# Sliding attention in a three-block network: one row of scores per query, the sink as a column, deeper buffers, the norm's scale moved into the rotation's tables

## The chip, the cores and the metric

The kernel is one program on one core of a Trainium2 chip. It has five engines that run their own instruction streams and meet only at semaphores: TensorE (PE; its weight loads are PEld), VectorE (DVE), ScalarE (ACT), GpSimd (POOL) and SyncE (SP, which here only starts the loads of weights). The metric is the device time of one execution in microseconds (us).

## The reference, cut to what matters

Three blocks in a row work on 256 tokens of width 1024. The change touches the third block, in which 16 meta tokens stand in front of the 256 (272 in all), and there the mixer of its second layer: attention in a sliding window, 16 query heads of 64, four heads of keys and values, and a sink (one learned number per head) in the softmax.

```python
def sink_softmax(s, mask, sink):
    s = jnp.where(mask, s.astype(jnp.float32), NEG_INF)
    m = jnp.maximum(jnp.max(s, axis=-1, keepdims=True), sink)
    p = jnp.exp(s - m)
    return p / (jnp.sum(p, axis=-1, keepdims=True) + jnp.exp(sink - m))

def swa_mixer(hn, w_q, sinks, w_out, k, v, cos, sin):     # hn = rmsnorm(h) * gain
    q = (hn @ w_q).reshape(B, L, N_KV_HEADS, GROUP, HEAD_DIM)
    q = (apply_partial_rope(q, cos, sin) * (HEAD_DIM ** -0.5)).transpose(0, 2, 3, 1, 4)
    ...
    mask = jnp.concatenate([
        jnp.ones((nB, WINDOW_3, N_META), dtype=bool),
        (j > i)[None] & (blk > 0),
        jnp.broadcast_to((j <= i)[None], (nB, WINDOW_3, WINDOW_3)),
    ], axis=-1)
    p = sink_softmax(s, mask, sink_b[None, :, :, None, None, None])
    o_real = jnp.einsum('bkgnqs,bknsd->bkgnqd', p.astype(v.dtype), v_band)
```

The window is 128. A query in the second half of the 256 tokens sees, of the first half's 128 keys, those with j > i, and of its own half's those with j <= i: for each query the two masks never take the same column, so the two halves together have exactly 128 visible keys, beside the 16 meta keys.

## The kernel before, in words

The whole network is a list of stages in `build`; each stage has one method per engine (`pe`, `act`, `dve`, `pool`), and the engines run the stages in order. Activations lie transposed, feature by token. Products with large weights are exact to fp32 by three fp32r products (`mm3`: high by high, low by high, high by low); every 128x1024 unit of weights is loaded by SP into one of 8 raw slots, its high part is copied by ACT (`W.hi`, tile `hi`, 5 slots in a ring, or a `spare` slot), and its low part is computed by DVE (`W.lo`) or, for every third unit, by POOL (`W.lo_pool`). Small products of attention are plain fp32.

A stage begins with an entry, which applies the last stage's update to `xT` and norms it. There are two kinds in play here. `Full`: eight tiles are updated (DVE, two operations each) and squared (ACT); PE sums the squares, DVE and POOL compute the inverse root, PE spreads it over the partitions; only then DVE makes x * gain * scale (tile `sq`), ACT its high part `hh` and DVE its low part `hl`, and the first product of the stage follows. `Lazy` (the entry of most feed-forward stages): `hh` and `hl` are made of x * gain as soon as a tile is updated, the products run on them, and the norm's sums and scale come after the first product, in the shadow; the scale is applied to the products.

`Swa` (from line 3678) is the stage that is changed; its entry is `Full`. Eight units of query weights give eight pairs of heads (u = 0 to 7). `first` computes two of them, `lin` one each in iterations 1, 3, 5, 7, 9 and 11 of the loop. A pair's query goes PE product, ACT (`query`, scale 1/8, tile `qs`), then the rotation (`Rope`): PE multiplies by a permutation, POOL multiplies `qs` by the cosines, DVE the permuted one by the sines, DVE adds (`rotated`, signal `rq`). Attention runs over 16 windows w: pair u = w // 2, half m = w % 2, both heads r of the pair at a time. The loop over i (`for i in range(21)`) is a software pipeline written out by hand; every engine takes its part of the windows in a fixed order:

- PE in iteration i: `scores(i)`, `lin` when it is due, `turn(i-3)` (transposes of the probabilities), the permutation, `values(i-5)`;
- ACT: copies of the products of window i-6 out (tile `sqr`), copies of the transposes of window i-4 out, `exps(i-1)`, `query`;
- DVE: `probs(i-2)`, `rowmax(i)`, `W.lo`, `rotated`, the low part of the output of window i-6 (tile `swal`, signal `ol`).

For m = 1 a row of scores has 272 columns (two halves and 16 meta keys), for m = 0 144. `rowmax` adds the mask for each head, takes the maximum, the maximum with the sink, its negative, and sink minus maximum: six instructions, in which each small one waits for the one before. `exps` takes the exponential of the sink and of two rows with their sums. `probs` adds the sink's term, takes the reciprocal and scales the two rows. The scores have two banks for each of two windows; the output of `values` has one bank, so that `values(w)` waits for `ol(w-1)`:

```python
        pe.wait_ge(*self.pta(w))
        if w:
            pe.wait_ge(*self.ol(w - 1))
```

The 16 meta queries go through a small path of their own (`meta_scores`, `meta_max`, `meta_probs`, `meta_turn`, `meta_values`). After the loop comes the output product (`Down`), whose first instruction waits for `ol(15)`.

Of the kernel before, what the change touches and what calls it, by code (L numbers as in the profile page):

```python
# [31 lines left out]
def table(sizes):  # L32
# [22 lines left out]
    ("chunk", 2), ("level", 320), ("mask64", 128), ("id64", 64), ("nlow", 64), ("nup", 64), ("tri128", 128), ("suf128", 128), ("swa", 272), ("cos", 272), ("sin", 272), ("turn", 128),  # L55
# [3 lines left out]
def constants():  # L59
# [216 lines left out]
class K:  # L276


    def __init__(self, nc, ctx, d, out):
# [19 lines left out]
        self.small, _ = self.place("small", 512)  # L299
        self.NA = (nc.sbuf_usable_end - self.at) // 4 // 16 * 16  # L300
        self.A, self.Aat = self.place("arena", self.NA)
        self.ps = [ctx.enter_context(nc.psum_tensor(f"ps{i}", [P, 512], F32)) for i in range(8)]
# [356 lines left out]
class Lazy:  # L659


    def __init__(self, K, T, prev, gain, j):
        self.K, self.T, self.prev = K, T, prev
        self.gain = lambda k: K.col(gain, j * 8 + k)
        self.hh, self.hl, self.sq, self.pr, self.rs = [
            K.sig(*a) for a in (("hh", 8), ("hl", 8), ("sq", 8), ("pair", 4), ("rstd", 1))]
# [2907 lines left out]
class Rope:  # L3574
# [10 lines left out]
    def pool(self, pool, j, src, t1):  # L3585
        pool.wait_ge(*self.qs(j))
        pool.tt(t1, src, self.K.c("cos"), ALU.mult).then_inc(self.t1.h, 1)

    def dve(self, dve, j, t2, bank):
        dve.wait_ge(*self.rm(j))  # L3590
        dve.tt(t2, bank[:, 0:T3], self.K.c("sin"), ALU.mult).then_inc(self.t2.h, 1)
        dve.wait_ge(*self.t2(j))
        dve.wait_ge(*self.t1(j))


class Shared(Mixer):
# [30 lines left out]
    def act(self, act):  # L3627
# [7 lines left out]
        act.act(self.V[:, 0, :], ps[0][:, 0:256], ACT.Copy)  # L3635
        act.act(self.V[0:16, 2, :], ps[7][0:16, 0:256], ACT.Copy).then_inc(self.va.h, 1)

    def dve(self, dve):
# [5 lines left out]
        for j in range(2):  # L3644
            t1, t2 = self.t1[:, j, :], self.t2[:, j, :]
            self.rope.dve(dve, j, t2, ps[4 + 2 * j])
# [8 lines left out]
    def pool(self, pool):  # L3655
# [6 lines left out]
        for j in range(2):  # L3662
            self.rope.pool(pool, j, self.fm[:, j, :], self.t1[:, j, :])
# [14 lines left out]
class Swa(Mixer):  # L3678

    def __init__(self, K, entry, exit_):
# [6 lines left out]
        self.S = buf(8 * T, 4, 2, T)  # L3689
        self.PT = buf(2 * 4 * P, 2, 4, P)  # L3690
        self.PM = buf(2 * 2 * P, 2, 2, P)
        self.qs, self.t1, self.t2 = [buf(2 * T, 2, T) for _ in range(3)]
# [5 lines left out]
        self.rq = sg("sw_q", 8)  # L3698
        self.sc, self.mx, self.es, self.ex, self.pr, self.tr, self.pta, self.pv, self.oh, self.ol = [
            K.sig(x, 16) for x in ("scores", "rowmax", "sink", "exps", "probs", "turned", "pta", "pv", "oh", "ol")]  # L3700
        (self.m0, self.m1, self.m2, self.m3, self.m4, self.m5, self.m6, self.m7, self.m8, self.mh) = [
            sg("sw_m" + str(i), 1) for i in range(10)]
        self.st = [[K.small[:, 64 * i + 16 * x:64 * i + 16 * x + 2] for x in range(3)] for i in range(4)]
        self.st2 = [K.small[0:16, 320 + 16 * x:336 + 16 * x] for x in range(3)]
        self.down = Down(K, T, "swa_out", self.mix, 8, lambda k: self.ol(2 * k + 1), spare=K.spare)
# [3 lines left out]
    KEYS = (((0, P), (T1, 16)), ((0, T3),))  # L3709
    WIDE = (144, 272)  # L3710
# [3 lines left out]
    def pe(self, pe):  # L3714
        K, ps, T = self.K, self.K.ps, T3
        self.entry.pe(pe)
        self.first(pe, self.u, (ps[7], ps[6]), K.HL, T, self.entry.hl)
# [3 lines left out]
        for i in range(21):  # L3721
            if i < 16:
                self.scores(pe, i)
            if i % 2 and i < 12:
# [5 lines left out]
            if i % 2 == 0 and 0 < i < 14:  # L3730
                j = (i + 2) // 2
                self.rope.pe(pe, j, self.qs[:, j % 2, :], self.product(j))
            if i > 4:
                self.values(pe, i - 5)
            if i == 13:
                self.meta_scores(pe)
            if i == 16:
                self.meta_turn(pe)
            if i == 18:
# [6 lines left out]
    def product(self, j):  # L3746
        return self.K.ps[4 + j if j < 2 else 7]

    def meta_scores(self, pe):
        K = self.K  # L3750
        pe.wait_ge(*self.rq(7))
        pe.wait_ge(*self.mx(12))
        for h in range(16):
            o = 64 * (h % 2)
            t = pe.mm(K.ps[h % 2][0:16, h // 2 * 16:h // 2 * 16 + 16], self.qT[o:o + 64, h // 2, T1:T3],
                      self.kD[o:o + 64, h // 4, T1:T3])
# [18 lines left out]
    def scores(self, pe, w):  # L3775
        K, u, m = self.K, w // 2, w % 2
        pe.wait_ge(*self.rq(u))
        if w > 1:
            pe.wait_ge(*self.mx(w - 2))
        if w == 14:  # L3780
            pe.wait_ge(*self.m1(0))
        for r in range(2):
            o, at = 64 * r, 0
            for c, n in self.KEYS[m]:
                t = pe.mm(K.ps[w % 2 * 2 + r][:, at:at + n], self.qT[o:o + 64, u, m * P:(m + 1) * P],
                          self.kD[o:o + 64, u // 2, c:c + n])
                at += n
        t.then_inc(self.sc.h, 1)

    def turn(self, pe, w):  # L3790
        K, u, m = self.K, w // 2, w % 2
# [3 lines left out]
        else:  # L3795
            pe.wait_ge(*self.rope.t2(1))
        for r in range(2):
            for c in range(m + 1):
                at = (r * (m + 1) + c) * P
                pe.tr(K.ps[4][:, at:at + P], self.S[:, w % 4, r, c * P:(c + 1) * P], K.ident)  # L3800
            c = P * (m + 1)
            t = pe.tr(K.ps[5][0:16, r * P:(r + 1) * P], self.S[:, w % 4, r, c:c + 16], K.ident)
        t.then_inc(self.tr.h, 1)

    def out(self, w):
        return self.K.ps[6][:, 0:P]

    def values(self, pe, w):
        K, u, m = self.K, w // 2, w % 2
        kv = u // 2 * 64  # L3810
        pe.wait_ge(*self.pta(w))
        if w:
            pe.wait_ge(*self.ol(w - 1))
# [383 lines left out]
```

## Time and profile before

| what | value |
|---|---|
| time, median of 3 runs | 3581.78 us (3574.05 to 3582.15) |
| time of the profiled execution | 3582.93 us |
| its span | 3581.1 us |
| mean granted TensorE clock | 0.925 of full |
| PE busy | 3283.6 us (92%) |
| DVE, ACT, POOL busy | 1808.7, 1526.3, 912.4 us |

The span is what the profiler saw from first to last instruction; 1.8 us of the time lie around it. Granted clock: TensorE runs at one of two levels, 1.2 GHz (0.50) and 2.4 GHz (1.00); a stretch between them was partly at either. All helper calls carry the line of the helper (L158 is `tt`, L162 `ts`, L166 `stt`, L172 `red`, L175 `act`, L178 `mm`, L186 `tr`), so operations are told apart by their tiles. A plain fp32 matmul shows as two records, a transpose and an fp32r matmul as one; some records are missing from the trace.

### The profile page before, as it was taken

Reading aid. Unit: us, or ns where it says so; the run is one execution under the profiler, and the core shown is the slowest. Engines: PE = TensorE matmul, PEld = TensorE weight load, DVE = VectorE, ACT = ScalarE, POOL = GpSimd, SP = SyncE. Lnnn points to the kernel's source line nnn. Section 1 sums busy time; section 2 is a strip of 40 time slices with the busy share of each in tenths; the row PEclk is TensorE's granted clock in tenths of the full one; section 3 lists DMA queues with packets and bytes.
Section 4 is the critical chain, followed back from the end, with each engine's and each line's share of the span. In section 5 each row is a group of like instructions: output and inputs, shape, how many; then the busy total and the mean of one; then the engine's idle time right before and its main releaser. Section 6 shows DMA issues by size and latency. Waiting matters only on the chain.

```text
span 3581.1 us, 63633 instructions
## 1 busy us (share of the span) xinstructions
PE 3283.6 (92%) x27126; PEld 3135.0 (88%) x27126; DVE 1808.7 (51%) x3157; ACT 1526.3 (43%) x2540; POOL 912.4 (25%) x474
## 2 busy tenths in 40 slices
PE   9998999989788999989969999999899979977998
PEld 9996999987678999988858899899799979975898
DVE  5446555558565454474655344544435454454443
ACT  5444444434124444356454344443334443432442
POOL 3221222322342323212202122222122222220222
PEclk9988999989898999989979999999899989986899
DMA  6541454544003555533414345354224524520353
GB/s 229 187 150 59 147 184 164 184 164 147 31 3 129 178 171 188 172 111 116 148 42 152 116 163 188 132 176 138 89 83 154 176 100 160 177 83 18 109 175 118
DMA packets 133385, 484.43 MB, mean 135 GB/s; under 512 B 14959, under 2 KB 17151, under 8 KB 132399
## 3 DMA queue, kind: packets, MB, share of 16 engines
q1 hardware_dynamic: 131120, 470.25, 38.9%
q0 software_dynamic: 1984, 10.12, 0.9%
q8 instruction: 214, 3.51, 0.4%
q14 instruction: 67, 0.55, 0.0%
HBM read 479.27 MB, written 1.05 MB: 134 GB/s over the span
## 4 chain that ended last, share of the span: by engine, by line
PE 81%; DVE 9%; ACT 5%; issue 3%; POOL 1%; DMA 0%; DVEq 0%; POOLq 0%; ACTq 0%
PE ps L178 80%; ACT hi L175 1%; DVE lo L158 1%; ACT arena L175 1%; PE ps L186 1%; DVE arena L158 1%; POOL small L158 1%; DVE tmp L166 1%; DVE yT L166 1%; DVE arena L166 1%; ACT L175 1%; DVE small L172 1%; ACT xT L175 0%; ACT hh L175 0%; DVE hl L158 0%
## 5 line engine op out<-in xcount | busy, mean ns | idle before, releaser
L178 PE MATMUL ps<-hh,lo 128*128 128x256 f32 (+1 forms) x4624 | 1342.8, 290 | 0.0
L178 PE MATMUL ps<-hh,hi 128*128 128x256 f32 (+1 forms) x4336 | 1273.9, 294 | 74.5 <-DVE hl L166 33.2
L178 PE MATMUL ps<-hl,hi 128*128 128x256 f32 (+1 forms) x4336 | 1261.1, 291 | 0.0
L158 POOL TENSOR_TENSOR lo<-raw,hi 128x1024 fp32r<-128x1024 f32 x271 | 687.3, 2536 | 1893.2 <-ACT hi L175 1893.1
L175 ACT ACTIVATE hi<-raw 128x1024 fp32r<-128x1024 f32 x814 | 852.5, 1051 | 462.8 <-PE ps L178 341.9
L158 DVE TENSOR_TENSOR lo<-raw,hi 128x1024 fp32r<-128x1024 f32 x543 | 699.0, 1290 | 603.3 <-ACT hi L175 582.5
L178 PEld LDWEIGHTS ps<-hh,hi 128*128 128x128 f32 x4336 | 851.1, 196 | 91.1 <-DVE hl L166 24.2
L178 PEld LDWEIGHTS ps<-hh,lo 128*128 128x128 f32 x4624 | 904.5, 196 | 0.0
L178 PEld LDWEIGHTS ps<-hl,hi 128*128 128x128 f32 x4336 | 849.2, 196 | 0.2
L178 PE MATMUL ps<-hfh,lo 128*128 128x256 f32 (+1 forms) x1760 | 499.7, 284 | 0.0
L178 PE MATMUL ps<-hfh,hi 128*128 128x256 f32 (+1 forms) x1520 | 431.2, 284 | 0.0
L178 PE MATMUL ps<-hfl,hi 128*128 128x256 f32 (+1 forms) x1520 | 430.9, 283 | 0.0
L178 PEld LDWEIGHTS ps<-hfh,lo 128*128 128x128 f32 x1760 | 331.6, 188 | 0.0
L178 PE MATMUL ps<-arena 64*64 64x64 f32 (+10 forms) x2992 | 257.6, 276 | 66.6 <-DVE sqr L158 18.0
L178 PEld LDWEIGHTS ps<-arena 64*64 64x64 f32 (+5 forms) x2992 | 193.1, 162 | 124.0 <-issue 40.2
L178 PEld LDWEIGHTS ps<-hfl,hi 128*128 128x128 f32 x1520 | 286.7, 189 | 0.0
L178 PEld LDWEIGHTS ps<-hfh,hi 128*128 128x128 f32 x1520 | 286.4, 188 | 0.0
L158 DVE TENSOR_TENSOR tmp<-tmp,ps 128x256 f32<-128x256 f32 (+1 forms) x220 | 94.0, 427 | 334.6 <-PE ps L178 313.8
L175 ACT ACTIVATE arena<-ps 128x256 f32<-128x256 f32 (+6 forms) x300 | 117.6, 412 | 292.3 <-PE ps L178 224.7
L175 ACT ACTIVATE hfh<-tmp 128x256 fp32r<-128x256 f32 (+1 forms) x220 | 93.0, 423 | 297.4 <-DVE tmp L158 295.9
L158 DVE TENSOR_TENSOR hfl<-tmp,hfh 128x256 fp32r<-128x256 f32 (+1 forms) x220 | 128.0, 582 | 125.8 <-ACT hfh L175 125.8
L175 ACT ACTIVATE tmp<-tmp 128x256 f32<-128x256 f32 (+1 forms) x176 | 74.8, 425 | 244.7 <-DVE tmp L158 244.7
(351 smaller groups left out, 3859.6 us busy)
## 6 DMA issues: line engine op xcount, KB each, us to landing
raw<-in_l_ffn_w_gate SPq DMA_DIRECT2D x88, 512.0 KB, 3.5
raw<-in_l_ffn_w_up SPq DMA_DIRECT2D x88, 512.0 KB, 4.0
raw<-in_l_ffn_w_down SPq DMA_DIRECT2D x88, 512.0 KB, 4.2
raw<-in_g SPq DMA_DIRECT2D x88, 512.0 KB, 3.3
raw<-in_u SPq DMA_DIRECT2D x88, 512.0 KB, 3.3
raw<-in_d SPq DMA_DIRECT2D x88, 512.0 KB, 3.3
raw<-in_ffn_w_gate SPq DMA_DIRECT2D x44, 512.0 KB, 4.3
raw<-in_ffn_w_up SPq DMA_DIRECT2D x44, 512.0 KB, 4.3
```

The source lines that it names most:

```text
L158: return self.e.tensor_tensor(o, a, b, op)
L166: return self.e.scalar_tensor_tensor(o, a, s, b, op0, op1)
L172: return self.e.tensor_reduce(o, a, AX_X, op)
L175: return self.e.activation(o, a, f, **kw)
L178: return self.e.matmul(o, a, b, start=first, stop=final, skip_group_check=loose)
L186: return self.e.transpose(o, a, ident)
```

## The change

- The entry of `Swa` becomes `Lazy`. `first` computes four query pairs at once, from banks 0 to 3; then come the norm's sums, two permutations, and `spread`. DVE multiplies the tables of cosines and sines by the norm's scale (tiles `cos`, `sin` of the stage), and the rotations use these. `lin` is left in iterations 5, 7, 9 and 11.
- Scores: the meta keys have columns of their own; for m = 1 the keys of the other half go to columns 256 to 383 of the bank. DVE adds the mask to both heads in one instruction and, for m = 1, writes the other half's scores over the masked columns (`copy_predicated`). Both halves' keys so share one row of 128. The sink stands as a column of the row (written once by POOL), so that one `tensor_reduce` with `negate` gives the negative maximum of both heads and the exponential's sum holds the sink's term.
- `probs`: a reciprocal and one multiplication over both heads. `turn`: three transposes for every window. For m = 1 the transposed probabilities are multiplied by one mask on DVE (`PN`) and by the other on POOL (`PB`), and `values` reads these.
- Buffers: 16 rows instead of 4 for scores, four for the transposes, four for `qs`, two output banks; `values(w)` waits for `ol(w-2)` and runs as `values(i-6)`; the loop has 23 iterations on PE and 24 on ACT and DVE.
- The stage `Shared` copies the meta values a second time (partitions 32 to 47). The constants grow from 272 to 288 + 128 columns for the masks. PSUM is one tensor of eight banks. The output product's last three units use spare slots of the stage's own.

```diff
-    keep = np.concatenate([j > i, j <= i, np.ones((P, 16), bool)], 1)
+    keep = np.concatenate([j <= i, np.ones((P, 32), bool), j <= i], 1)
     put("swa", np.where(keep, 0.0, BIG))
+    put("swab", j > i)
...
+        act.act(self.V[32:48, 2, :], ps[7][0:16, 0:256], ACT.Copy)
...
     def pe(self, pe):
-        self.entry.pe(pe)
-        self.first(pe, self.u, (ps[7], ps[6]), K.HL, T, self.entry.hl)
+        self.first(pe, self.u, ps[0:4], K.HL, T, self.entry.hl)
+        self.entry.norm.sums(pe, [(2 * i, self.entry.pr(i)) for i in range(4)])
         K.enter.have(pe)
         for j in range(2):
             self.rope.pe(pe, j, self.qs[:, j, :], self.product(j))
-        for i in range(21):
+        self.entry.norm.spread(pe)
+        for j in (2, 3):
+            pe.wait_ge(*self.rope.t2(j - 2))
+            self.rope.pe(pe, j, self.qs[:, j, :], self.product(j))
+        for i in range(23):
             if i < 16:
                 self.scores(pe, i)
-            if i % 2 and i < 12:
+            if i % 2 and 4 < i < 12:
...
-            if i > 4:
-                self.values(pe, i - 5)
+            if i > 5 and i - 6 < 16:
+                self.values(pe, i - 6)
...
-        for r in range(2):
-            o, at = 64 * r, 0
-            for c, n in self.KEYS[m]:
-                t = pe.mm(K.ps[w % 2 * 2 + r][:, at:at + n], self.qT[o:o + 64, u, m * P:(m + 1) * P],
+        parts = ((0, 16), m * P, P), ((P, 0), T1, 16), ((256, 256), 0, P)
+        for at, c, n in parts[:2 + m]:
+            for r in range(2):
+                o = 64 * r
+                t = pe.mm(self.K.ps[w % 2 * 2 + r][:, at[r]:at[r] + n], self.qT[o:o + 64, u, m * P:(m + 1) * P],
                           self.kD[o:o + 64, u // 2, c:c + n])
...
         for r in range(2):
-            for c in range(m + 1):
-                at = (r * (m + 1) + c) * P
-                pe.tr(K.ps[4][:, at:at + P], self.S[:, w % 4, r, c * P:(c + 1) * P], K.ident)
-            c = P * (m + 1)
-            t = pe.tr(K.ps[5][0:16, r * P:(r + 1) * P], self.S[:, w % 4, r, c:c + 16], K.ident)
+            pe.tr(b[:, r * P:(r + 1) * P], self.row(w)[:, 176 * r:176 * r + P], self.K.ident)
+        t = pe.tr(b[0:48, 256:384], self.row(w)[:, P:176], self.K.ident)
...
-        if w:
-            pe.wait_ge(*self.ol(w - 1))
+        if m:
+            pe.wait_ge(*self.mn(u))
+            pe.wait_ge(*self.mb(u))
+        if w > 1:
+            pe.wait_ge(*self.ol(w - 2))
...
+        dve.wait_ge(*self.entry.norm.spr(0))
+        dve.mark(dve.tt(self.cos, K.c("cos"), self.entry.norm.out, ALU.mult))
+        dve.tt(self.sin, K.c("sin"), self.entry.norm.out, ALU.mult).then_inc(self.tb.h, 1)
+        dve.wait_ge(*self.tb(0))
...
+    def masked(self, e, u, to, mask, done):
+        e.wait_ge(*self.pta(2 * u + 1))
+        if u > 1:
+            e.wait_ge(*self.pv(2 * u - 3))
+        e.tt(to[:, u % 2, :].rearrange("p (r t) -> p r t", r=2),
+             self.PT[:, (2 * u + 1) % 4, :].rearrange("p (r t) -> p r t", r=2),
+             bc_mid(self.K.c(mask), 2), ALU.mult).then_inc(done.h, 1)
...
-        for r in range(2):
-            dve.mark(dve.tt(self.S[:, w % 4, r, 0:n], K.ps[w % 2 * 2 + r][:, 0:n], K.c("swa")[:, 272 - n:272], ALU.add))
-        dve.turn()
-        dve.mark(dve.red(mx, self.S[:, w % 4, :, 0:n], ALU.max))
-        dve.turn()
-        dve.mark(dve.tt(mx, mx, sink, ALU.max))
-        dve.turn()
-        dve.mark(dve.ts(mx, mx, -1.0, None, ALU.mult))
-        dve.turn()
-        dve.tt(e, sink, mx, ALU.add).then_inc(self.mx.h, 1)
+        b = K.banks[:, w % 2 * 2:w % 2 * 2 + 2, :]
+        dve.mark(dve.tt(self.two(S, 160, 144), b[:, :, 0:144],
+                        K.c("swa").rearrange("p (r c) -> p r c", r=2), ALU.add))
+        dve.turn()
+        if m:
+            dve.mark(dve.e.copy_predicated(self.two(S, 176, P), bc_mid(K.c("swab").bitcast(mybir.dt.uint32), 2),
+                                           b[:, :, 256:384]))
+            dve.turn()
+        dve.e.tensor_reduce(mx, self.two(S, 159, 145), AX_X, ALU.max, negate=True).then_inc(self.mx.h, 1)
...
-        lambda p: Swa(K, Full(K, T3, p, "norm_gains_3", 8), rms("norm_gains_3", 9, False, False, K.Hf)),
+        lambda p: Swa(K, Lazy(K, T3, p, "norm_gains_3", 8, False), rms("norm_gains_3", 9, False, False, K.Hf)),
```

## Rows read from the trace of the kernel before

**Rows 1.** The page, part 4: the chain that ended last, by engine.
```profile
PE 81%; DVE 9%; ACT 5%; issue 3%; POOL 1%; DMA 0%; DVEq 0%; POOLq 0%; ACTq 0%
```
**Rows 2.** Windows: stretch, its length, busy us (instructions) by engine, PEclk, DMA share, GB/s.
```profile
3165.28:3188.85 23.57, 18.96 (x101) 18.33 (x102) 13.46 (x34) 6.86 (x17) 1.20 (x2) 0.56 0.00 1
3188.85:3219.93 31.08, 20.65 (x129) 16.78 (x128) 22.21 (x61) 13.03 (x38) 8.60 (x6) 0.84 0.19 68
3219.93:3264.19 44.26, 35.80 (x206) 26.18 (x205) 21.94 (x75) 15.40 (x54) 4.59 (x4) 0.81 0.11 37
3264.19:3324.60 60.41, 46.68 (x249) 27.73 (x247) 19.47 (x73) 15.87 (x58) 0.76 (x1) 0.53 0.03 9
...
3312.03:3319.52 7.49, 7.49 (x53) 5.07 (x52) 0.29 (x1) 1.28 (x4) 0.00 (x0) 0.50 0.01 2
```
**Rows 3.** The chain in order of time, stage's entry and two `lin`: start, us, what.
```profile
3175.81 1.21 POOL small L158 x2
...
3177.07 1.77 PE ps L178 x6
...
3207.09 4.55 PE ps L178 x24
...
3216.81 3.31 PE ps L178 x24
```
**Rows 4.** Waits of PE, 3219 to 3325 us: total us, times, longest.
```profile
PE ps L178 <- DVE swal L158: 17.8, 11, 2.6
PE ps L186 <- ACT arena L175: 3.9, 6, 1.0
```
**Rows 5.** Timeline of DVE and PE in the next stage's `Lazy` entry (four units).
```profile
3356.90 0.50 DVE L166 SCALAR_TENSOR_TENSOR yT<-yT,cols,ps 128x272 f32<-128x272 f32 x1 [2.41 <-PE ps L178]
...
3373.58 2.50 PE L178 MATMUL ps<-cst,sq 128*128 128x1 f32 x22
```
**Rows 6.** Groups by shape, DVE, ACT, POOL: count, busy us, mean ns, idle before.
```profile
L158 DVE TENSOR_TENSOR lo<-raw,hi 128x1024 fp32r<-128x1024 f32 x543 | 699.0, 1290 | 603.3 <-ACT hi L175 582.5
...
L158 DVE TENSOR_TENSOR arena<-ps,cst 128x272 f32<-128x272 f32 x24 | 9.8, 435 | 17.8 <-PE ps L178 17.8
L158 DVE TENSOR_TENSOR arena<-arena 128x272 f32<-128x272 f32 x8 | 4.0, 500 | 0.6 <-POOL arena L158 0.4
L172 DVE TENSOR_REDUCE small<-arena 128x2 f32<-128x288 f32 x8 | 3.6, 453 | 0.3
...
L3520 DVE COPY_PREDICATED arena<-cst,ps 128x128 f32<-128x128 uint32 x8 | 2.0, 298 | 7.6 <-PE ps L178 7.6
...
L175 ACT ACTIVATE arena<-ps 128x256 f32<-128x256 f32 x8 | 3.0, 378 | 0.0
...
L158 POOL TENSOR_TENSOR lo<-raw,hi 128x1024 fp32r<-128x1024 f32 x3 | 7.1, 2354 | 41.3 <-ACT hi L175 41.3
L158 POOL TENSOR_TENSOR arena<-arena,cst 128x272 f32<-128x272 f32 x8 | 7.0, 880 | 33.4 <-ACT arena L175 33.4
```
**Rows 7.** Timeline of PE late in the loop: start, us, what [idle before <-releaser].
```profile
3280.91 3.08 PE L178 MATMUL ps<-arena 128*64 128x128 f32 x40 [1.38 <-DVE swal L158]
3284.57 1.04 PE L178 MATMUL ps<-arena 64*128 64x128 f32 x8 [0.58 <-DVE arena L158]
...
3288.26 4.60 PE L178 MATMUL ps<-arena 128*64 128x128 f32 x16 [1.17 <-DVE swal L158]
3292.84 1.09 PE L186 MATMUL ps<-cst,arena 128*128 128x128 f32 x4
3296.53 2.54 PE L178 MATMUL ps<-arena 128*64 128x128 f32 x8 [2.61 <-DVE swal L158]
3300.04 1.51 PE L186 MATMUL ps<-cst,arena 128*128 128x128 f32 x6 [0.97 <-ACT arena L175]
...
3320.30 3.36 PE L178 MATMUL ps<-arena 128*64 128x128 f32 x12 [0.78 <-DVE swal L158]
```
**Rows 8.** Timeline of DVE beside a running low-part subtraction on POOL.
```profile
3213.75 1.73 DVE L158 TENSOR_TENSOR small<-small,rows 128x2 f32<-128x2 f32 x1
```

More of the change, by code:

```diff
@@ L298, in __init__ @@
         self.tmp = p3(self.place("tmp", 4 * T3)[0][:, :], 4)
-        self.small, _ = self.place("small", 512)
+        self.small, _ = self.place("small", 464)
         self.NA = (nc.sbuf_usable_end - self.at) // 4 // 16 * 16
         self.A, self.Aat = self.place("arena", self.NA)
-        self.ps = [ctx.enter_context(nc.psum_tensor(f"ps{i}", [P, 512], F32)) for i in range(8)]
+        self.banks = ctx.enter_context(nc.psum_tensor("ps", [P, 8, 512], F32))
+        self.ps = [self.banks[:, i, :] for i in range(8)]
         self.ident, self.ones = self.c("ident"), self.c("ones")
@@ L3751, in meta_scores @@
         pe.wait_ge(*self.rq(7))
[L3752 to L3756, printed above, removed]
+        for r in range(2):
+            for u in range(8):
+                o, h = 64 * r, 2 * u + r
+                t = pe.mm(K.ps[7][0:16, h * 16:h * 16 + 16], self.qT[o:o + 64, u, T1:T3],
+                          self.kD[o:o + 64, u // 2, T1:T3])
+            if r == 0:
+                pe.mark(t)
+                pe.turn()
         t.then_inc(self.m0.h, 1)
@@ L3827, in act @@
         self.entry.act(act)
-        for j in range(2):
-            self.query(act, j, ps[7 - j])
-        for i in range(22):
-            if i > 5:
-                w = i - 6
+        for j in range(4):
+            self.query(act, j, ps[j])
+        for i in range(24):
+            if i > 6 and i - 7 < 16:
+                w = i - 7
                 act.wait_ge(*self.pv(w))
@@ L3949, in probs @@
-        t.then_inc(self.pr.h, 1)
+        s = self.two(self.row(w), 160, 144)
+        dve.tt(s, s, bc(den, 144), ALU.mult).then_inc(self.pr.h, 1)
     def meta_max(self, dve):
@@ L3983, in pool @@
         K, W = self.K, self.K.W
-        pool.wait_ge(*K.enter.loaded())
+        K.enter.all(pool)
         K.enter.tables(pool)
         K.enter.have(pool)
+        if self.u:
+            pool.wait_ge(*W.used(self.u - 1))
+        rows = self.S[:, 0:16 * 304].rearrange("p (u m c) -> p m u c", m=2, c=304)
+        pool.e.memset(self.S[:, 0:16 * 304].rearrange("p (w c) -> p w c", c=304)[:, :, 144:160], 0.0).then_inc(self.pad.h, 1)
+        pool.wait_ge(*self.pad(0))
+        sinks = K.row("swa_sinks_3").rearrange("p (u r) -> p r u", r=2)
+        for r in range(2):
+            for m in range(2):
+                t = pool.cp(rows[:, m, :, self.SINK[r]], sinks[:, r])
+        t.then_inc(self.snk.h, 1)
         self.entry.pool(pool)
+        self.entry.norm.power(pool)
+        W.lo_pool(pool, self.u + 6)
+        pool.wait_ge(*self.tb(0))
         for j in range(8):
+            self.rope.pool(pool, j, self.qs[:, j % 4, :], self.t1[:, j % 4, :], self.cos)
             W.lo_pool(pool, self.u + j + 6)
-            self.rope.pool(pool, j, self.qs[:, j % 2, :], self.t1[:, j % 2, :])
+            if j > 3:
+                self.masked(pool, j - 4, self.PB, "suf128", self.mb)
+        for u in range(4, 8):
+            self.masked(pool, u, self.PB, "suf128", self.mb)
         self.down.pool(pool)
```

177 lines of the change are left out of this document (91 added, 86 removed).

## The prediction, made before the changed kernel was run

> **What bounds the kernel now.** I read the page first: the chain that ended last lies for 81% on PE [rows 1], so time comes off only where PE waits, runs at the low clock, or has work that goes away. The stage that changes runs from the first update of `xT` (3165.28 us) to the first product of `Down` (3324.60): 159.3 us, which I cut with the windows view into an entry, the loop up to the end of `lin` in iteration 5 (3219.93), up to the end of the last `lin` in iteration 11 (3264.19), and a tail without dense products [rows 2]. The reader should see that the four parts have different limits. The entry, 23.6 us, is a round trip: PE sums the squares as the updates go on, then come inverse root and spread (1.21 and 1.77 us) [rows 3], then DVE makes the normed tiles before a product can start. In the loop, PE is busy 36 of 44 us and 47 of 60 us. The waits view says what the rest is: 17.8 us in eleven waits for `swal`, that is for `ol(w-1)`, and 3.9 us for ACT's copies of the transposes [rows 4]. The wait for `ol` is a ring: `values(w)` fills the one output bank, PE does `scores`, DVE does the whole of `rowmax` for these scores first (its order is written by hand) and only then `ol(w)`, which frees the bank. The tail is PE at half clock: 0.53 on average, and 0.50 even in 7.5 us in which PE never stopped [rows 2]. So there every product counts double.
>
> **The change, part by part.** I lay out a new time line from 3165.28, where the stage starts as before.
>
> *Entry.* The next stage has the new kind of entry, with four units too: from its first update (3356.90) to the start of the norm's sums (3373.58) are 16.7 us [rows 5]. That puts the end of the four products at 3182.0, with two more pairs of heads done than before had at 3188.85. Then the sums 2.5 us [rows 5], variance 0.3, inverse root 1.2 and spread: 1.8 at half clock [rows 3], 0.9 at full; I take 1.3: 3187.3. DVE's two tables at 0.44 (PSUM by constant, 272 columns [rows 6]) end at 3188.2. Then four rotations: POOL is behind them with 0.8 to 0.88 each [rows 6], and the last addition follows: 3192.2. All this is on the path, because `rowmax(0)` stands behind the four rotations in DVE's order.
>
> *First iterations.* New `rowmax`: addition over 288 columns 0.46 (the 272 wide one is 0.435), reduction 0.45, so 0.95 with the gaps; for m = 1 also the predicated copy of 256 columns, 0.43 (0.298 for 128, and another 128 columns at the slope of about 1 ns of the additions) [rows 6]: 1.4. `probs`: a reciprocal on two columns and one multiplication over 288 (0.50 for the 272 wide addition, some of it waiting [rows 6]): 0.5 together. In DVE's order: `rowmax(0)` to 3193.2, `rowmax(1)` to 3194.6, two low-part subtractions of 1.25 (1.29 on average over the kernel [rows 6]; iteration 1 now has both) to 3197.1, `probs(0)` and `rowmax(2)` to 3198.5, `probs(1)` and `rowmax(3)` to 3200.5. `scores(5)` needs that last one; then `lin` of iteration 5, which after a wait costs 4.55 and not 3.31 [rows 3]: it ends at about 3205.6. Before that point was 3219.93. Saved: **14.3 us** (12 to 17: the clock in the four products, and DVE's gaps).
>
> *Iterations 6 to 11.* Three pairs of windows took 44.26 us, 14.8 a pair, clock 0.81 [rows 2]. New work of PE for a pair, from rows at half clock [rows 7]: `values` 2.54 (m = 0, eight records) and 3.36 (m = 1, twelve), unchanged. `turn`: four transposes take 1.09, six 1.51, so 0.21 for one more, and three take 0.88, twice 1.76 in place of 2.60. `scores` m = 0: eight records 1.04, at most as before. `scores` m = 1: 4.60 less 3.36 is 1.24 for two products of 272 columns; the new one has four of 128 and two of 16, which I put between 1.0 and 2.0, at 1.5. Together 10.2 at half, 5.1 at full clock; with `lin` (3.31 at full) and a permutation (one product of 272 columns, an estimate from the 1.24 for two: 0.9 at half, 0.45 at full) 8.9 at full. At the old mix of clocks (0.81) that is 10.9. The ring is gone: `values(w)` waits for `ol(w-2)`, which has a whole iteration to come. What is late next is `pta`: ACT does the output's copy and two copies (0.38 for the longest [rows 6]) before `turn` may go on, about 0.95 us from the end of `values`, and PE has only `scores` to fill it: 0.3 a window, 0.6 a pair. 11.5 a pair, 34.5 for three. Saved: **9.8 us** (16 if the clock holds full: 8.9 + 0.6 + 0 = 9.5 a pair; 4 if it falls to 0.70: 8.9 / 0.70 + 0.6 = 13.3).
>
> *Tail.* At half clock, from the end of the last `lin`: eight `turn` 7.0; six `values` of m = 1 and five of m = 0 (windows 5 to 15, one window more than before, since `values` now runs an iteration later) 20.2 + 12.7; four `scores` 2 × 1.04 + 2 × 1.5 = 5.1; one permutation 1.0; the meta path 0.6 for its scores (3.08 less 2.54 [rows 7]), an estimated 2.2 for its other products (as many, some wider); the first `turn` and `values(5)` still at full clock, less 2.1; then waits for `pta`: 0.3 in four iterations, 0.97 in three without `scores` (as now [rows 7]), 4.1; and 0.95 from the last `values` to `Down`. Sum 51.8. Now it is 60.4. Saved: **8.6 us**, I take 8 (4 to 13: `scores` dearer, a mask late, or a part at full clock).
>
> *What costs nothing.* DVE has about 3.0 + 3.1 us of work a pair (two `rowmax` 2.35, two `probs` 1.0, `rotated` 0.9, `PN` 0.45, `ol` 0.6, a subtraction 0.8) against PE's 11: PE covers it. ACT has under 6. POOL's masks (0.88 at most) for window 2u+1 wait for ACT's copy in iteration 2u+5 and are needed in iteration 2u+7, so two windows of PE hide them. The sinks are written by POOL in the entry, where it waits for DVE. More constants load in the first blocks' shadow. The second copy of the meta values in `Shared` is on the path: ACT makes it before the copy that PE waits for, **+0.3 us**.
>
> *A rule beside the rows.* A DVE operation on two columns took 1.73 us [rows 8], longer than a reduction of 288 columns (0.453), while a subtraction of 2.35 us ran on POOL [rows 6]. The Trainium skill (SBUF — State Buffer, "Who interferes with whom") says that a DVE instruction with two SBUF inputs and a GpSimd one that reads SBUF exclude each other for the whole instruction; the trace agrees with 1.73 us. By that rule eight new POOL masks could stop DVE for up to 8 × 0.88 = 7.0 us; without it for nothing. Neither changes the sum while PE covers DVE. By itself: the Trainium skill (TensorEngine Tiling, "Key Properties") says that row tiles work independently, by which the interleaved heads' scores would come out near the 1.0 end; no row here shows it.
>
> **Sum.** 14.3 + 9.8 + 8.0 - 0.3 = 31.8 us. The profiled execution took 3582.93 us (1.8 around its span), 1.2 above the median shown; so the new one should be about 3551 and the median **3550 us**, 0.9% less.
>
> **Rivals.**
> - *The clock stays at half in the whole loop.* Dense products lift it; two of six `lin` leave the loop, and the entry's pauses are shorter but still there. The tail at 0.50 with PE at work [rows 2] speaks for it; that a `lin` ran in 3.31 us and the mean there is 0.81 [rows 2, 3] speaks against. Then: four products 8 us longer, `lin` of iteration 5 1.2 longer, a pair 6.6 + 0.9 + 10.2 + 0.6 = 18.3, three of them 55 against 44.3. 14.3 - 9.2 - 10.7 + 8 - 0.3 = 2 saved: 3580 us, no change. Chance 7%.
> - *The clock holds at full through most of the loop*, because the waits of 1 to 2.6 us go. 14.3 + 16 + 8 + up to 10 in the tail: 3533 to 3543 us. The 7.5 us at 0.50 speak only against rising, not against staying. Chance 15%.
> - *DVE becomes the bound (the slower side).* The row views are strided, the predicated copy reads PSUM, and POOL's masks block it. It decides when DVE needs more than PE's 11.5 a pair; to eat all 32 us over eight pairs it must need 15.5, that is 9.4 more than I count, 1.2 us on each of eight operations. One blocked by a subtraction for 1.7 us in a pair is what rows 8 show, not five. At 17 a pair: 3594 us. Chance 4%.
> - *A part of the gain is missing* (rotations or `pta` longer, scores at 2.0): 15 to 22 saved, 3560 to 3567 us. Chance 14%.
>
> **Chances and range.** My forecast, 3543 to 3558, has 60%. The range of 8 in 10 takes in most of the third and second rival: 3534 to 3568. 0.3% is 10.7 us, about what a measurement of this kernel can tell from no change. Faster by more: forecast, full clock and smaller gain, 88% (I give one point to no change); within: 8%; slower: 4%.
>
> **What would show it.** The first product of the stage under the updates of `xT`, and the last of the four units' near 3182; `lin` of iteration 5 ending near 3205; no wait of PE for `swal` in the loop; `turn` with three transposes, 0.9 us at half clock; the tail near 52 us at 0.50 to 0.55; DVE groups of 0.45 us in place of the small ones. It would be wrong if the span from 3182 to the first `scores` is much over 10 us, if PE waits for DVE's maxima or for a mask in every iteration, or if the granted clock in the middle is under 0.7.

## The result and the profile after

Four runs of the changed kernel have a median of 3532.24 us (3527.84 to 3535.96), four of the kernel before 3579.14 us. The ratio is 0.9864 with a 95% interval of 0.9850 to 0.9877: 1.4% faster, 47 us on medians, where 31.8 had been forecast. The direction is right, the size is 1.5 times the forecast, and the time lies 1.8 us under the range of 3534 to 3568.

The windows view of the changed kernel, cut at the same events as before: first update of `xT`, end of the four units, end of `lin` in iteration 5, end of the last `lin`, first product of `Down`. Columns as in [rows 2]; the second part is given in two pieces, split at 3190.30, and the last two rows split the tail behind the fall of the clock.

```profile
3163.60:3179.44 15.84, 13.48 (x97) 13.49 (x98) 11.69 (x28) 7.67 (x18) 0.00 (x0) 0.83 0.01 2
3179.44:3190.30 10.86, 8.99 (x46) 6.19 (x45) 4.60 (x13) 5.39 (x8) 7.49 (x8) 0.65 0.52 193
3190.30:3207.40 17.10, 14.11 (x90) 12.31 (x89) 12.87 (x26) 5.39 (x24) 1.84 (x1) 0.53 0.00 1
3207.40:3235.06 27.66, 25.94 (x207) 20.25 (x205) 17.18 (x42) 12.72 (x47) 6.70 (x7) 1.00 0.17 58
3235.06:3278.30 43.24, 39.48 (x258) 24.35 (x257) 17.66 (x52) 13.41 (x54) 4.96 (x6) 0.64 0.04 13
3235.06:3249.40 14.34, 13.62 (x127) 9.24 (x126) 9.93 (x28) 7.32 (x30) 3.03 (x4) 0.93 0.12 39
3249.40:3278.30 28.90, 25.86 (x132) 15.11 (x133) 7.73 (x26) 6.09 (x24) 1.93 (x2) 0.50 0.00 1
```

The middle ran at 1.00 where it had 0.81 [rows 2], and the tail kept the high clock for its first 12 us. By parts, against the forecast's own time line:

| part | before | forecast | after | saved |
|---|---|---|---|---|
| first update to end of `lin` in iteration 5 | 54.6 | 40.3 | 43.8 | 10.8 (14.3 forecast) |
| to the end of the last `lin` | 44.3 | 34.5 | 27.7 | 16.6 (9.8) |
| tail, to `Down` | 60.4 | 52.4 | 43.2 | 17.2 (8.0) |
| stage | 159.3 | 127.2 | 114.7 | 44.6 |

The two spans differ by 47.0 us (3581.1 and 3534.1). The other 2.4 lie outside the stage, 1.7 of them ahead of it; profiled executions differ there by more than that (last section). The waits of PE in the loop of the changed kernel, columns as in [rows 4]:

```profile
PE ps L187 <- ACT arena L176: 4.8, 9, 1.1
PE ps L179 <- DVE small L3981: 1.4, 2, 1.2
PE ps L187 <- DVE arena L159: 1.2, 1, 1.2
```

`swal` is gone from the list. What is left is `pta` (nine waits, the longest 1.1 us) and, in the loop's first iterations, three waits for DVE's first maxima and probabilities. The timeline of PE late in the loop and in the tail, to be read against [rows 7]:

```profile
3235.32 2.50 PE L179 MATMUL ps<-arena 128*64 128x128 f32 x20
3238.14 0.52 PE L187 MATMUL ps<-cst,arena 128*128 128x128 f32 x3 [0.33 <-ACT arena L176]
...
3245.16 4.22 PE L179 MATMUL ps<-arena 128*64 128x128 f32 x52
3249.31 0.90 PE L187 MATMUL ps<-cst,arena 128*128 128x128 f32 x3
3250.14 3.39 PE L179 MATMUL ps<-arena 128*64 128x128 f32 x12
3254.41 0.88 PE L187 MATMUL ps<-cst,arena 128*128 128x128 f32 x3 [0.88 <-ACT arena L176]
3255.22 2.54 PE L179 MATMUL ps<-arena 128*64 128x128 f32 x8
...
3264.51 12.86 PE L179 MATMUL ps<-arena 128*64 128x128 f32 x72
```

Three transposes take 0.88 us at half clock and 0.52 or less at full; twelve records of `values` take 3.39 (3.36 before) and eight 2.54, as before. The last row of the timeline is 12.9 us of such products without a pause, all of it in a stretch at 0.50. The level had fallen 12.3 us after the last `lin` (full for 0.86 of the 14.34 us at 0.93), with no wait of PE longer than 0.33 us since. The groups by shape of DVE and POOL, for the prices that the forecast had to estimate:

```profile
L159 DVE TENSOR_TENSOR arena<-arena,small 128x288 f32<-128x288 f32 x16 | 7.3, 458 | 0.6
L3981 DVE TENSOR_REDUCE small<-arena 128x2 f32<-128x290 f32 x16 | 7.3, 455 | 0.6
...
L159 DVE TENSOR_TENSOR arena<-ps,cst 128x288 f32<-128x288 f32 x16 | 7.2, 451 | 4.8 <-PE ps L179 4.7
L159 DVE TENSOR_TENSOR arena<-arena 128x272 f32<-128x272 f32 x8 | 5.9, 733 | 0.7 <-POOL arena L159 0.5
...
L3978 DVE COPY_PREDICATED arena<-cst,ps 128x256 f32<-128x256 uint32 x8 | 3.6, 446 | 0.3
```
```profile
L159 POOL TENSOR_TENSOR arena<-arena,cst 128x256 f32<-128x256 f32 x8 | 6.4, 802 | 28.3 <-ACT arena L176 28.3
```

They came out as priced (0.451, 0.446, 0.455 and 0.458 us; POOL's masks 0.80). The one that didn't is the rotation's addition: 0.733 us on average, mainly because one of the eight was held (2.12 us; the first took 0.91, the last four 0.44). The timelines of POOL and DVE at that place:

```profile
3186.33 3.31 POOL L159 TENSOR_TENSOR arena<-arena 128x272 f32<-128x272 f32 x4 [0.41 <-DVE arena L159]
3189.59 2.55 POOL L159 TENSOR_TENSOR lo<-raw,hi 128x1024 fp32r<-128x1024 f32 x1
```
```profile
3190.32 2.12 DVE L159 TENSOR_TENSOR arena<-arena 128x272 f32<-128x272 f32 x1
3192.36 0.44 DVE L159 TENSOR_TENSOR arena<-ps,cst 128x288 f32<-128x288 f32 x1
3192.84 0.45 DVE L3981 TENSOR_REDUCE small<-arena 128x2 f32<-128x290 f32 x1
```

The last addition waits until POOL's subtraction ends at 3192.14, and `rowmax(0)`, the head of the chain that starts the loop, stands behind it.

### The profile page after: what moved, and what is told of

Read it like the earlier page. It is cut to its first block, busy times and chain, and to the rows that moved or that the text cites. A ratio compares the mean times of both kernels' runs of the same rounds, so it can differ in the third digit from the quotient of the medians.

```text
span 3534.1 us, 63583 instructions
## 1 busy us (share of the span) xinstructions
PE 3263.6 (92%) x27134; PEld 3123.4 (88%) x27134; DVE 1798.0 (51%) x3076; ACT 1520.4 (43%) x2525; POOL 921.1 (26%) x487
## 4 chain that ended last, share of the span: by engine, by line
PE 82%; DVE 9%; ACT 5%; issue 3%; POOL 1%; DMA 0%; SPq 0%; DVEq 0%; POOLq 0%; ACTq 0%
PE ps L179 81%; ACT hi L176 1%; ACT arena L176 1%; DVE lo L159 1%; PE ps L187 1%; POOL small L159 1%; DVE arena L159 1%; DVE tmp L167 1%; DVE arena L167 1%; DVE yT L167 1%; ACT L176 1%; DVE small L173 1%; DVE tmp L164 0%; ACT hh L176 0%; ACT xT L176 0%
## 5 line engine op out<-in xcount | busy, mean ns | idle before, releaser
L179 PE MATMUL ps<-arena 64*64 64x64 f32 (+13 forms) x3056 | 252.7, 272 | 46.8 <-DVE sqr L159 17.9
L179 PEld LDWEIGHTS ps<-arena 64*64 64x64 f32 (+7 forms) x3056 | 194.5, 162 | 100.0 <-issue 39.0
```

The costliest lines, as they stand in the source:

```text
L179: return self.e.matmul(o, a, b, start=first, stop=final, skip_group_check=loose)
```

## The experiments

Times of different batches are compared through the runs of the kernel before that each batch had (ratio, 95% interval). As the part ahead of the stage varies from one profiled execution to the next, the effect on the stage is read from each trace, from the first update of `xT` to the first product of `Down`: 159.3 us before, 114.7 us changed. The first theory: one output bank made a ring of waits (a circle in which each engine waits for the other), the waits pulled the clock down, and the clock that came back with their removal is what the forecast missed. Its rival: the shorter softmax and transposes made PE denser.

**One output bank again.** The changed kernel, with this edit:

```diff
-        return self.K.ps[5 + w % 2][:, 0:P]
+        return self.K.ps[5][:, 0:P]
...
-        if w > 1:
-            pe.wait_ge(*self.ol(w - 2))
+        if w:
+            pe.wait_ge(*self.ol(w - 1))
```

> The changed kernel with one output bank again: values(w) waits for ol(w-1), all else as changed. Theory 1 (the ring through the one output bank made PE wait, and these waits pulled the clock down; its removal is what held the clock at 1.00 between the lin of iterations 5 and 11 and for 14 us of the tail): the clock of the middle falls back to 0.75 to 0.85, a pair of windows takes 12.5 us or more in place of 9.2, and the kernel loses 18 to 28 us of its 47: 3550 to 3560. Theory 2 (the clock held because the merged row makes transposes and the DVE chain shorter, so PE is denser anyway): the middle stays at 0.95 or more and the time at 3532 to 3540.

Median 3562.74 us, ratio 0.9952 (0.9937 to 0.9967); the stage took 144.5 us. Windows of the middle and the tail, and PE's waits there:

```profile
3200.18:3242.00 41.82, 34.27 (x206) 26.23 (x205) 17.45 (x42) 12.73 (x47) 6.69 (x7) 0.76 0.11 38
3242.00:3300.88 58.88, 46.41 (x259) 28.12 (x257) 17.93 (x52) 13.43 (x54) 4.82 (x6) 0.54 0.03 10
```
```profile
PE ps L179 <- DVE swal L159: 16.4, 11, 3.1
```

With shorter transposes, one reduction and the merged row all in place, middle and tail are within 2.5 us of those of before (44.3 and 60.4), and the clock is as low (0.81 and 0.53 before). 29.8 of the 44.6 us are gone with one wait. The loss is a little larger than the 18 to 28 us of the theory (30.5 us on medians), and the rival is refuted.

**The bank freed first.** The kernel before, with one block of DVE moved ahead of `rowmax`; nothing else of the change:

```diff
             if 1 < i < 18:
                 self.probs(dve, i - 2)
+            if i > 5:
+                w = i - 6
+                ...
+                dve.tt(self.mix[1][:, w // 2, c], self.out(w), self.mix[0][:, w // 2, c].bitcast(F32),
+                       ALU.subtract).then_inc(self.ol.h, 1)
             if i < 16:
                 self.rowmax(dve, i)
```

> The kernel before with one edit: DVE frees the output bank (ol of window i-6) ahead of rowmax(i) and not after it. It opens the ring without touching scores, softmax, transposes, buffers or entry. Theory 1: PE's 17.8 us of waits for swal mostly go and the clock of the middle rises above 0.9: 12 to 22 us faster, 3557 to 3567. Theory 2: the waits move to the next late signal and the clock stays at 0.8: at most 5 us faster, 3574 to 3580.

Median 3553.25 us, ratio 0.9925 (0.9908 to 0.9942): 27 us faster than the kernel before, above the 12 to 22 expected. The stage took 130.8 us. Windows and waits of the middle and the tail:

```profile
3211.04:3240.80 29.76, 28.50 (x206) 21.20 (x205) 21.59 (x75) 15.42 (x54) 4.61 (x4) 1.00 0.16 55
3240.80:3287.00 46.20, 39.95 (x247) 24.00 (x245) 19.01 (x72) 15.89 (x58) 0.77 (x1) 0.62 0.04 12
```
```profile
PE ps L186 <- ACT arena L175: 4.8, 8, 1.0
PE ps L178 <- DVE swal L158: 2.1, 3, 0.9
```

The same instructions as before, 206 records on PE in the middle, take 29.8 us in place of 44.3 (the tail: 46.2 for 60.4). Half of these 14.5 us is idle time of PE (8.5 before, 1.3 now); the other half is busy time, 28.5 us for 35.8 with the same records, because the clock is 1.00 and was 0.81. The windows of the kernel before at the first `ol` wait that cost it the clock show the order of events:

```profile
3219.93:3224.00 4.07, 3.65 (x30) 2.45 (x28) 2.64 (x9) 3.23 (x10) 0.76 (x1) 1.00 0.41 129
3224.00:3226.00 2.00, 0.26 (x2) 0.00 (x0) 1.86 (x7) 0.00 (x0) 0.00 (x0) 1.00 0.00 0
3226.00:3230.00 4.00, 3.86 (x17) 2.16 (x17) 0.95 (x5) 1.16 (x5) 0.00 (x0) 0.63 0.02 4
```

PE stands for 1.88 us, then takes up `values`, and the level drops in the middle of them.

The edit takes `ol` past more than `rowmax`. DVE's order of before had `rowmax`, the low-part subtraction of a weight unit (odd iterations) and the rotation (even ones) ahead of it, and the subtraction waits for ACT. The chain of the kernel before shows it at the second wait for `ol` (2.45 us):

```profile
3235.41 0.95 ACT hi L175
3236.38 1.23 DVE lo L158
3237.61 0.21 DVE swal L158
```

The two runs show that the ring costs the clock. They don't show how: the ring lets PE stand, and it also moves the dense products of `lin` further apart. A wait alone need not do it: with the subtractions moved to iteration 5 (below) there is a wait of 1.59 us in the middle, and the middle stands at 1.00 throughout; and in the tail of the changed kernel the level fell without a long wait. That wait, and the window of that middle:

```profile
3205.31 0.39 PE L179 MATMUL ps<-hh,hi 128*128 128x272 f32 x1 [1.59 <-DVE arena L159]
```
```profile
3198.49:3227.81 29.32, 26.00 (x206) 20.23 (x205) 19.13 (x42) 12.85 (x47) 9.99 (x8) 1.00 0.17 55
```

**The old entry.** The changed kernel with `Full` in place of `Lazy`, four units first as changed, the tables as plain copies of the constants:

```diff
-        self.first(pe, self.u, ps[0:4], K.HL, T, self.entry.hl)
-        self.entry.norm.sums(pe, [(2 * i, self.entry.pr(i)) for i in range(4)])
+        self.entry.pe(pe)
+        self.first(pe, self.u, ps[0:4], K.HL, T, self.entry.hl)
...
-        dve.mark(dve.tt(self.cos, K.c("cos"), self.entry.norm.out, ALU.mult))
-        dve.tt(self.sin, K.c("sin"), self.entry.norm.out, ALU.mult).then_inc(self.tb.h, 1)
+        dve.mark(dve.cp(self.cos, K.c("cos")))
+        dve.cp(self.sin, K.c("sin")).then_inc(self.tb.h, 1)
```

> The changed kernel with the entry of before: the tiles are normed before the first products, the tables are plain copies of the constants; four units first, as changed. Theory (entry is worth what the prediction's time line says, 12 us of the wait ahead of the products less 5 us of sums, root and spread behind them): 6 to 9 us slower than the changed kernel, 3538 to 3542, nothing changed in the loop. Rival (the entry also sets the clock of what follows, because PE idles longer ahead of the first product): 12 us or more, with the four products partly at 0.50.

Median 3537.53 us, ratio 0.9885 (0.9870 to 0.9900). The stage took 119.4 us, 4.7 more than changed, a little less than the theory's 6 to 9. The windows of the four units and of the stretch behind them:

```profile
3165.30:3194.43 29.13, 24.52 (x151) 23.88 (x152) 13.88 (x36) 7.95 (x18) 1.21 (x2) 0.67 0.01 2
3194.43:3217.17 22.74, 16.79 (x100) 13.03 (x100) 16.35 (x33) 10.63 (x32) 8.15 (x6) 0.62 0.26 92
```

The units end 13.3 us later after the first update (29.1 for 15.8), but 5.2 us come back in the stretch behind, which no longer holds sums, root and spread (22.7 for 28.0), and 3.4 in the tail, where the clock fell later (39.9 at 0.73 for 43.2 at 0.64). Middle and its clock are unchanged (27.7 at 1.00). The rival is refuted for the middle: the entry doesn't set its clock. Why the same products of the tail kept the high level for longer here is open; without these 3.4 us the old entry costs 8.1 us, inside the theory's 6 to 9.

**Dense products in the tail.** The changed kernel; PE also makes products that nothing reads (`hh` by itself), into a bank of scores that is free:

```diff
+            if 12 <= i < 21:
+                pe.wait_ge(*self.mx(min(i - 1, 14)))
+                for k in range(6):
+                    pe.mm(ps[(i + 1) % 2 * 2 if i < 16 else 0][:, 0:T], K.H[:, k % 8, 0:P], K.H[:, k % 8, 0:T])
             if 2 < i < 19:
                 self.turn(pe, i - 3)
```

> The changed kernel with six dense fp32r products of 128x128 by 272 columns, whose result nothing reads, in each of the iterations 12 to 20 of PE, behind scores and ahead of the transposes. They cost 0.75 us an iteration at full clock, some of it inside waits for pta. Theory 1 extended (the clock in the tail falls because the tail's products, 64 columns or 16 rows of weights, count little, and dense ones would hold it): the clock of the tail stays over 0.9 and the tail shrinks from 43.2 us to 33 to 37: 6 to 10 us faster than the changed kernel. Rival (six short products in 2.5 to 3.5 us don't hold it): the tail at 0.50 from the same place, and 5 to 9 us slower.

Median 3528.81 us, ratio 0.9854 (0.9838 to 0.9871). The stage took 107.9 us, 6.8 less. The window of the tail:

```profile
3236.50:3272.98 36.48, 35.48 (x314) 25.26 (x311) 17.58 (x52) 13.44 (x54) 4.84 (x6) 1.00 0.05 16
```

54 more products, and the tail is shorter: it never left the high level. In the total the gain is within the noise of two batches (0.9854 beside 0.9864); the trace settles it.

**The same on the kernel before, with the bank freed first.**

> The kernel before with only two edits: ol ahead of rowmax, and the six dense products in iterations 12 to 20. If the clock in the tail is held by the dense products whatever the rest of the stage looks like, the tail of 46.2 us with clock 0.62 goes to 38 to 41 us at 1.00: 5 to 8 us faster than with ol ahead alone, 3545 to 3548. Rival (only the changed kernel's denser stage lets it hold): no change or slower than 3553.

Median 3537.23 us, ratio 0.9878 (0.9865 to 0.9892): two small edits of the kernel before bring 44 us. The window of its tail:

```profile
3243.80:3280.20 36.40, 34.83 (x301) 24.42 (x299) 18.97 (x72) 15.79 (x58) 0.77 (x1) 1.00 0.04 15
```

The tail fell from 46.2 to 36.4 us, 9.8 us, above the 5 to 8 expected, and the stage to 121.0; the other 6 us or so by which this median lies under that of the bank alone (3553.25) are not in the stage. Structure and row widths are the old ones, and 54 products were added: the tail is shorter by its clock alone.

**Three in place of six, and one burst.** Three products in each of iterations 13 to 20; and twelve in iteration 14 alone, where the clock of the changed kernel falls.

> The changed kernel with three dense products an iteration in 13 to 20 alone, beside the run with six in 12 to 20 (tail 36.5 us at 1.00, stage 107.9). If three are enough: tail 34 to 36 us. If not: the clock falls in the tail, 43 us or more.

> The changed kernel with twelve dense products in iteration 14 alone, where its trace shows the clock falling (3247 us, in the 16 column products of the meta queries). Theory (without dense products the tail's own cannot hold the clock, so the fall only comes later): the clock falls 3 to 8 us after the burst, the tail is 40 to 43 us. Rival (the small products of the meta queries are the one cause, and past them the tail holds): tail at 1.00 to the end, 32 to 35 us.

Three: median 3524.11 us, ratio 0.9839 (0.9824 to 0.9854), stage 105.2 us. The tail is 33.7 us at 1.00, 2.7 less than with six, with 24 products in place of 54. The burst: 3532.28 us, ratio 0.9860 (0.9844 to 0.9877), stage 112.4 us, tail 41.0. Windows, first of the run with three, then of the burst:

```profile
3230.87:3264.61 33.74, 31.81 (x282) 21.36 (x281) 17.49 (x52) 13.44 (x54) 4.98 (x6) 1.00 0.05 17
```
```profile
3250.00:3252.00 2.00, 1.32 (x9) 0.73 (x8) 1.90 (x7) 0.92 (x5) 0.00 (x0) 1.00 0.00 0
3252.00:3254.00 2.00, 1.80 (x10) 0.96 (x10) 1.90 (x7) 0.85 (x5) 0.00 (x0) 0.86 0.00 0
3254.00:3256.00 2.00, 1.12 (x6) 0.66 (x5) 1.40 (x5) 0.70 (x3) 0.56 (x1) 0.50 0.00 0
```

The theory behind the burst was that the tail's own products can't hold the clock; its rival, that the 16 column products of the meta queries are the one cause of the fall. After the burst these small products pass at 1.00, and the level falls at about 3253.4 (full for 0.72 of the second window), 8.4 us behind the burst, after a wait for `pta` of 0.88 us. So they are not the one cause; without further dense products the fall only comes later. The theory had 3 to 8 us and 40 to 43 us of tail. The dense products differ from the tail's own in the size of their weights, their columns and their type at once; which of these keeps the level wasn't run apart.

**The subtractions moved.** In the changed kernel DVE's two subtractions of iteration 1 and POOL's behind rotation 3 lie on the chain into the loop.

```diff
-            if i % 2 and i < 12:
+            if i % 2 and 4 < i < 12:
                 W.lo(dve, self.u + (i + 3) // 2 + 6)
...
-            W.lo_pool(pool, self.u + j + 6)
+            if j != 3:
+                W.lo_pool(pool, self.u + j + 6)
```

> The changed kernel with the low-part subtractions moved out of the stretch before lin of iteration 5: DVE's two of iteration 1 go to iteration 5, POOL's third-unit one goes from behind rotation 3 to behind rotation 4. Theory: the trace of the changed kernel shows DVE's last rotation add at 2.12 us in place of 0.5 while POOL's subtraction of 2.55 us ran, and 2.27 us of DVE's two between rowmax(1) and probs(0), both on the chain; with them gone the stretch of 27.8 us from the last of the four units to the end of lin of iteration 5 shrinks by 3 to 4 us: 3527 to 3530. Rival (PE at half clock is the limit there, busy 23 of 27.8 us): at most 1 us.

> The moved subtractions and the six dense products in iterations 12 to 20 together. If both are independent the gains add: 6.7 us of the tail as seen in the stage of the filler run, and 3 to 4 us: 3520 to 3524, the tail at a granted clock of 1.00. Rival (one undoes the other): no better than either alone.

> The changed kernel with the moved subtractions, DVE's now one each in iterations 5 and 7 and two each in 9 and 11. In the run that moved them all to iteration 5 the stretch before lin of iteration 5 fell from 27.8 to 24.8 us, but the next one grew by 1.6 us. Theory (DVE was late there): that 1.6 us goes, the stage takes 111 us in place of 114.7, 3 to 4 us less than the changed kernel. Rival (POOL's order is what grew it): the stage stays at 112.5.

> The same with three dense products an iteration in iterations 13 to 20. If three hold the clock as six did, the tail is 34 to 36 us at 1.00, the stage about 104 us: 10 us less than the changed kernel, 3520 to 3524. If they don't, the tail is 43 to 46 us, partly at 0.50.

Moved to iteration 5: 3530.47 us, ratio 0.9869 (0.9850 to 0.9887), stage 112.5 us; with six dense products 3526.16 us, 0.9841 (0.9826 to 0.9855), stage 106.6. Neither total is apart from the run that it builds on; by the stages the gains nearly add (2.2 and 5.9, where the dense products alone gave 6.8). The first fell short of the 3 to 4 us expected, since 3.0 us came off ahead of the end of `lin` of iteration 5, but the middle grew from 27.7 to 29.3; the second missed its 3520 to 3524 us. Spread as `W.lo(dve, self.u + {5: 7, 7: 8, 9: 11, 11: 13}.get(i, 0))`: 3528.64 us, ratio 0.9854 (0.9839 to 0.9868), stage 111.7 us. The stretch from the last of the four units to the end of `lin` of iteration 5 in this last run, and the middle:

```profile
3171.92:3196.72 24.80, 22.12 (x129) 17.93 (x130) 15.36 (x40) 10.74 (x32) 6.83 (x7) 0.59 0.21 84
3196.72:3224.37 27.65, 25.93 (x207) 20.22 (x205) 18.14 (x41) 12.74 (x47) 9.21 (x8) 1.00 0.18 58
```

24.8 us in place of 27.8 (3179.60 to 3207.40 in the changed kernel: here the stretch starts where the last unit's product ends, 0.16 us behind the start of the sums), and the middle back at 27.7: 3.0 us, as expected. With three dense products on top it is the fastest version: 3518.49 us, ratio 0.9827 (0.9812 to 0.9842), stage 102.2 us, tail 33.7 us at 1.00. That beats the changed kernel (0.9850 to 0.9877) clearly.

**Dense products early too.** On top of the run with the subtractions in iteration 5 and six dense products in the tail, six in each of iterations 0 to 5 as well.

> As the last, and six dense products also in each of iterations 0 to 5 (into the bank that values has free until iteration 6). If the clock of 0.57 between the four units and lin of iteration 5 is what makes that stretch long, it rises to 0.8 or more and 3 to 6 us more go: 3515 to 3520. Rival (the stretch is the chain DVE, ACT, DVE, and PE only waits, so that products there cost their time once they no longer fit in waits): 0 to 4 us slower than without them.

Median 3538.80 us, ratio 0.9876 (0.9858 to 0.9893). It is a miss on both sides: 3515 to 3520 us were expected, at worst 4 us more than without them, and the median is 12.6 us above theirs (3526.16). The trace is of the fastest of the four executions (3526.48; the others took 3537.78 to 3540.50), so it shows only a part of the loss. In it the stretch up to the end of `lin` of iteration 5 is longer, and the middle loses its clock. Windows of the two:

```profile
3172.09:3201.75 29.66, 27.81 (x165) 22.98 (x166) 16.23 (x39) 10.62 (x32) 6.83 (x7) 0.65 0.19 70
3201.75:3232.87 31.12, 28.69 (x206) 22.66 (x205) 19.13 (x42) 12.85 (x47) 10.00 (x8) 0.89 0.16 52
```

At half clock each of the 36 products cost about twice, more than the waits could hide; the clock rose only near the end of the stretch (0.65 in the mean, for 0.59) and fell again in the middle. The stage took 113.3 us, against 106.6 without them. Why it fell in the middle, which holds 1.00 in every other run here without the ring, is open, and so is what the three slower executions lost.

## Why the prediction was wrong

**The step that failed** is the clock of the middle: "At the old mix of clocks (0.81) that is 10.9". The sum of work was right, 8.9 us a pair at full clock and 0.6 of waits for `pta`, which is 9.5; the pairs took 9.2. But 0.81 was not a property of these products. It was what the ring through `ol` left of the clock, and the forecast had just taken this ring away. The two runs that touch only the ring show it from both sides: 0.76 with it, 1.00 without. This term was 6.8 us too small (16.6 for 9.8).

**The tail** failed for the same reason, "At half clock, from the end of the last `lin`". The high level came through the first 12 us of it; what lies behind its fall was as priced (0.88, 2.54 and 3.39 us). The reading that 7.5 us of uninterrupted work stood at 0.50 [rows 2] was true (12.9 us of it did in the changed kernel) and led astray: these products didn't raise the level, but for a while they kept it. The forecast's rival said just that, with a chance of 15% and 3533 to 3543 us, and its mechanism is what happened; its tail term, "up to 10", measured 9.2 above the 8.0. The range ended at 3534 although a rival reached below it. That the time fell under both is partly chance: 2.4 us of the 47 lie outside the stage, and the stage's 44.6 us alone, taken from 3581.78, would give 3537 us. What the forecast missed is in the stage: 44.6 us for 32.1, by 6.8 and 9.2 too little for the clock in middle and tail, less 3.5 in the first part.

**The first part** was 3.5 us too short: 43.8 for 40.3. The units took 15.8 us (16.7 forecast), and without the held addition the rotations would have ended 27.2 us after the first update (26.9). Then 1.6 us went for that addition, held by POOL's subtraction. The rule beside the rows had described such a hold, for the masks, and the forecast called it covered: "Neither changes the sum while PE covers DVE". In the loop PE covers DVE; ahead of it nothing does. The rest is `scores(5)`, 1.6 us at half clock where the line leaves 0.55 between `rowmax(3)` and `lin`, and `lin`, 5.2 for 4.55. The Trainium skill (SBUF — State Buffer, "Who interferes with whom") is borne out once more: POOL's subtraction of 2.55 us began first, and the DVE addition, with both inputs in SBUF, came out at 2.12 us and ended 0.3 us behind it.

**The other steps.** No wait for `swal`, transposes of 0.88 us, groups of 0.45 us on DVE, no wait for a mask: as forecast. `scores` for m = 1 was put at 1.5 between 1.0 and 2.0: twelve records take 1.65 us at half clock. The 0.3 us for the second copy in `Shared` can't be told apart: profiled executions differ by more ahead of the stage.

**The rivals.** Half clock in the whole loop: refuted by 1.00. DVE as the bound: refuted, it was busy 17.2 of 27.7 us in the middle. A missing part of the gain: only in the first 3.5 us.

**Where the change's 44.6 us come from**, by undoing or doing one part: about 29 the ring (29.8 by undoing, 28.5 alone on the kernel before), 4.7 the entry (8.1 without the tail's change of clock). The remaining 7 to 11 are the merged row, the shorter transposes and the two units that move out of the loop together; they weren't run apart.

## What to carry to other kernels

A wait on TensorE can be paid twice: once as idle time, and again in what follows if the clock falls behind it. In the middle of this stage the ring cost 7.2 us of idle time and 7.3 us of longer products. Not every wait does that, and the clock can fall without one. So when a change removes waits, the work behind them must be priced at both levels, and a mean granted clock from the old trace must not be carried over. Look for rings through a single buffer: one engine's order (here a softmax step, a weight subtraction or a rotation ahead of the small operation that frees the bank) can be mended by moving one instruction, which here brought more than half of what the whole rewrite did (28.5 of 44.6 us of the stage); and where a stretch has only small plain products, a few dense ones in its waits can be worth more than they cost (tail 33.7 us with 24 of them, 43.2 without).

## What the runs showed of the hardware

- TensorE's clock stayed at 1.00 through a tail of small plain fp32 products with dense fp32r products in each of its iterations up to 20: 33.7 us with three, 36.5 us with six. Without them it fell to 0.50 after 12.3 us, PE having waited for no more than 0.33 us at a time. At 0.50, 7.5 us [rows 2] and 12.9 us (changed kernel) of the small ones without a pause didn't raise it.
- The level fell about 1 us behind a wait of 1.88 us in the kernel before, but a wait of 1.59 us in the run with the subtractions moved to iteration 5 passed at 1.00 (middle 29.3 us at 1.00). The fall hangs on more than the length of one wait.
- Dense products in the waits of the stretch ahead, where the clock was low (0.59), didn't help: with 36 of them it took 29.7 us for 24.8, and the next 31.1 for 29.3.
- The same instructions ahead of the stage took 3156.2, 3159.3 and 3165.3 us in three profiled executions (the kernel before and its two edits, alike up to there). What changes a few us in one stage is to be read inside that stage; what makes this variation wasn't found.
